# Two-layer hybrid decoder, hand-over from mixer to experts: first head's queries projected from the unscaled state

## What is computed

```python
ada = (c_act @ ada_w[l] + ada_b[l])[:, None, :]
sh1, sc1, g1, sh2, sc2, g2 = jnp.split(ada, 6, axis=-1)
h = rms_norm(x, norm_mix_g[l]) * (1.0 + sc1) + sh1
x = x + g1 * hybrid_mixer(h, ...)
h = rms_norm(x, norm_ffn_g[l]) * (1.0 + sc2) + sh2
x = x + g2 * peer_ffn(h, peer_w_query[l], peer_sub_keys[l], peer_u[l], peer_v[l])

def peer_ffn(h, w_query, sub_keys, u_tab, v_tab):
    q = (xt @ w_query).reshape(T, PEER_HEADS, 2, PEER_DHALF)
    s = jnp.einsum('thpd,pkd->thpk', q, sub_keys).astype(jnp.float32)
    s_a, i_a = lax.top_k(s[:, :, 0], PEER_TOPK)
    s_b, i_b = lax.top_k(s[:, :, 1], PEER_TOPK)
    cand_s = (s_a[..., :, None] + s_b[..., None, :]).reshape(T, PEER_HEADS, n_cand)
    top_s, pos = lax.top_k(cand_s, PEER_TOPK)
    idx = jnp.take_along_axis(cand_i, pos, axis=-1)
    gate = jax.nn.softmax(top_s, axis=-1).astype(h.dtype)
    ...
        u = u_tab[ib]
        act = jax.nn.gelu(jnp.einsum('thkd,td->thk', u, xb), approximate=False)
        return jnp.einsum('thk,thkd->td', gb * act, v_tab[ib])
```

## Time and profile before

| | us |
|---|---|
| median of 3 runs | 2156.43 |
| lowest, highest | 2154.32, 2159.74 |
| profiled execution: time | 2158.78 |
| profiled execution: span of the profile | 2157.0 |
| mean granted TensorE clock | 0.972 |
| bytes moved by DMA | 713.12 MB |
| of these gathered rows | 536.90 MB |

### The profile page before, as it was taken

The page is one execution under the profiler, slowest core; times in us unless marked ns, Lnnn a source line. Parts: engine busy times, 40 slices in busy tenths (PEclk is TensorE's granted clock), DMA queues, the critical chain, the costliest instruction groups (busy, mean ns, idle before and its releaser), DMA issues.

```text
span 2157.0 us, 21974 instructions
## 1 busy us (share of the span) xinstructions
PE 1880.6 (87%) x6340; PEld 1094.4 (51%) x6340; DVE 1481.6 (69%) x4053; ACT 685.5 (32%) x1905; POOL 629.6 (29%) x608
## 2 busy tenths in 40 slices
PE   4999999988888888877799999998978879788776
PEld 3677777654434334433277777775534334334332
DVE  6676686776766767766636676776766766766774
ACT  1222332233333333333322332241333333333332
POOL 5000000144444444444300000002444445444442
PEclk9999999999999999999999999999999999999999
DMA  9855553299999999999986544336999999999997
GB/s 370 326 186 204 215 220 125 114 399 422 419 421 421 421 415 422 409 420 418 411 302 228 205 178 168 127 127 263 400 421 421 418 420 407 422 419 414 406 421 299
DMA packets 118818, 713.12 MB, mean 331 GB/s; under 512 B 13104, under 2 KB 17456, under 8 KB 51120
## 3 DMA queue, kind: packets, MB, share of 16 engines
q0 software_dynamic: 73728, 536.90, 60.2%
q1 hardware_dynamic: 44976, 174.97, 21.6%
HBM read 710.78 MB, written 1.05 MB: 330 GB/s over the span
## 4 chain that ended last, share of the span: by engine, by line
PE 46%; DMA 27%; DVE 15%; issue 4%; ACT 3%; POOL 2%; SPq 2%; DVEq 0%; POOLq 0%; ACTq 0%
DMA wall<-in_peer_uv,idx 23%; PE PS L1192 15%; PE PS L945 11%; PE PS L950 8%; DVE wall L1257 6%; PE PS L955 5%; DMA braw<-in_ada_rows 2%; POOL wall L623 2%; PE PS L1166 2%; ACT M L823 1%; PE PS L992 1%; DVE pos L1742 1%; ACT wgt L816 1%; DVE ts L1739 1%; PE PS L965 1%
## 5 line engine op out<-in xcount | busy, mean ns | idle before, releaser
L1192 PE MATMUL PS<-wall,M 128*128 128x512 f32 x2032 | 954.2, 619 | 214.4 <-ACT M L823 214.0
L1257 DVE CUSTOM_DVE_ANT_0 wall<-wall,tok 128x1024 f32<-128x1024 f32 x512 | 604.7, 1223 | 361.2 <-DMA wall<-in_peer_uv,idx 361.2
L623 POOL DMA_INDIRECT wall<-in_peer_uv,idx x512 | 569.1, 1111 | 714.6 <-PE PS L1192 509.8
L1192 PEld LDWEIGHTS PS<-wall,M 128*128 128x128 f32 x2032 | 384.8, 197 | 744.9 <-issue 412.0
L809 ACT ACTIVATE dg<-dg 128x2 f32<-128x2 f32 x254 | 51.6, 203 | 760.7 <-DVE dg L1257 760.7
L945 PE MATMUL PS<-hT,wall 128*128 128x256 f32 x1120 | 247.9, 380 | 1.3 <-DMA wall<-in_w_in 1.3
L945 PEld LDWEIGHTS PS<-hT,wall 128*128 128x128 f32 x1120 | 211.6, 190 | 31.5 <-ACT M L706 1.7
L565 POOL TENSOR_SCALAR rsb<-ms 128x4 f32<-128x4 f32 (+2 forms) x22 | 6.5, 296 | 756.7 <-DVE ms L1257 755.5
L950 PE MATMUL PS<-wall,hT 128*128 128x512 f32 x512 | 224.7, 592 | 0.2 <-ACT M L692 0.2
L823 ACT ACTIVATE M<-turn,wgt 128x128 f32<-128x128 f32 x508 | 176.2, 394 | 24.1 <-ACT wgt L816 0.7
L950 PEld LDWEIGHTS PS<-wall,hT 128*128 128x128 f32 x512 | 96.1, 190 | 109.3 <-issue 108.5
(11 more groups left out here) (277 smaller groups left out, 1870.8 us busy)
## 6 DMA issues: line engine op xcount, KB each, us to landing
wall<-in_w_in SPq DMA_DIRECT2D x112, 704.0 KB, 9.8
braw<-in_ada_rows SPq DMA_DIRECT2D x72, 512.0 KB, 4.2
wall<-in_w_out SPq DMA_DIRECT2D x2, 4096.0 KB, 14.8
wall<-in_peer_uv,idx POOLq DMA_INDIRECT x512
wall<-in_ada_rows SPq DMA_DIRECT2D x6, 1024.0 KB, 12.4
wall<-in_w_in SPq DMA_DIRECT2D x16, 384.0 KB, 11.0
mix<-in_peer_w_query SPq DMA_DIRECT2D x6, 1024.0 KB
wall<-in_w_in SPq DMA_DIRECT2D x16, 320.0 KB, 9.4
```

The lines of the kernel that those rows point to most:

```text
L623: nc.gpsimd.indirect_dma_start(out=pair_rows[b][s], out_offset=None, in_=uv_rows, in_offset=bass.IndirectOffsetOnAxis(ap=idx[i % 2][:, k:k ...
L1192: ins = mm(bank(B_ACC + 2 * t + hf), diag[:, b, s, :], pair_rows[b][s][:, D + hf * 512:D + (hf + 1) * 512], start=(i == FIRST_TILE[t] and ...
L1257: return v.tensor_tensor_reduce(out=o, in0=a, in1=b, scale=1.0, scalar=0.0, op0=ALU.mult, op1=ALU.add, accum_out=acc)
```

## The change

1. **Columns of a and b.** A new tile `acol` collects, during the mixer, the scale, the shift and the scale of the second norm as columns, two small DVE copies in each `block_out`. (`ccol` is where they were made for the rows `ada`.)
2. **The shift's share.** In `last_step` PE multiplies the shift column with the first head's query matrix (`q0c`, two columns, 16 matmuls of one moving column each); ACT copies them out; later two matmuls spread q0c @ keys over all tokens, in the free half of the bank of the turned keys (`s_shift`).
3. **First head's queries.** PE transposes `xs` as added (L1180), without the reciprocal root; ACT scales each 128x128 block by the scale column as it copies (`raw_evac`). DVE's `best_first` multiplies the scores by the token's root and adds the shift's share. The normed rows are made as before, and `turn_state(0)` with `state_evac(0)` now comes after the whole output projection, for the second head.
4. **The last head.** ACT makes the exponentials before the last sigmoid; DVE's `gates` are split, with the part that needs the sigmoid (`recur_gains`) after `squares`; on PE `levels` stand ahead of `transpose_tok(2)`, six chunks of `out_proj(0, 1)` follow the recurrence, and two chunks (not five) of `out_proj(1, 0)` stand ahead of the hand-over.
5. **Scratch by last use.** The tiles in `mix` are laid out so that a 1 MB third is free after the scores, after the gates, and at the end; four of the five late query matrices are loaded earlier.
6. **First sums.** `expert_sum(0)` comes ahead of the second head's key scores and `gate_rows`, and `expert_sum(1)` ahead of tile 1's transposes; the queries of tile 1 come one group later, and their copies on ACT too.

The diff, cut to its core:

```diff
+        acol = sb("acol", [P, 3 * KC])
+        q0c = sb("q0c", [P, 2])
...
+                sp.wait_ge(s_A, HEADS * (l + 1))
+                load_wq(l, 2, s_ahead)
+                sp.wait_ge(s_gated, l + 1)
+                load_wq(l, 3, s_ahead)
+                load_wq(l, NAHEAD + 2, s_ahead)
                 if l + 1 == DEPTH:
                     load_gain(final_g)
+                sp.wait_ge(s_y_rest, l + 1)
+                load_wq(l, HEADS - 1, s_ahead)
                 sp.wait_ge(s_mix, mixed(l) + HEADS)
-                for h in (*range(2, HEADS - 2), HEADS - 1):
-                    load_wq(l, h, s_ahead)
+                load_wq(l, NAHEAD + 1, s_ahead)
...
+                    if n is None:
+                        act.wait_ge(s_q0c, l + 1)
+                        nc.scalar.activation(q0c[:], bank(B_O)[:, 0:2], ACT.Copy).then_inc(s_q0cev, 1)
+                        nc.scalar.activation(e4[jm][:, :, 3, :], last_unit()[:, :, 1, :], ACT.Sigmoid).then_inc(s_zev, 1)
...
+                def raw_evac():
+
+                    for half in range(2):
+                        act.wait_ge(s_tp, NTP * l + 10 + half)
+                        for k in range(4 * half, 4 * half + 4):
+                            i = nc.scalar.activation(hT[:, k, 0:P], bank(B_H[0][half])[:, k % 4 * P:(k % 4 + 1) * P], ACT.Copy,
+                                                     scale=acol[:, 2 * KC + k:2 * KC + k + 1])
+                        i.then_inc(s_hTa, 1)
+
+                raw_evac()
                 query_evac(0, 0, s_q0, l + 1, s_q0ev)
                 turn_evac(KC - 2, 1, 12)
                 turn_evac(KC - 1, 1, 13)
+                state_evac(0)
...
                 route_exp(0)
+                weigh(0)
                 query_evac(1, 0, s_q1, l + 1, s_q1ev)
...
+                    pe.wait_ge(s_r[1], 16 * l + 16)
+                    for a in range(2):
+                        for k in range(KC):
+                            i = mm(bank(B_O)[:, a:a + 1], wqv[0][:, k, a * P:(a + 1) * P], acol[:, KC + k:KC + k + 1],
+                                   start=(k == 0), stop=(k == KC - 1))
+                    i.then_inc(s_q0c, 1)
                     pe.wait_ge(s_hTa, NHTA * l + 4)
                     pe.wait_ge(s_wo, 16 * (l + 1))
                     out_proj(0, 0, range(4))
+                    pe.wait_ge(s_q0cev, l + 1)
+                    levels(m, jm)
+                    turn_weights(m)
                     pe.wait_ge(s_zev, UNITS * (H0 + HEADS))
                     pe.wait_ge(s_mix, mixed(l) + 6)
                     transpose_tok(2)
-                    levels(m, jm)
-                    turn_weights(m)
                     pe.wait_ge(s_hTa, NHTA * l + 5)
                     out_proj(0, 0, (4, 5))
                     attend(m, jm)
-                    out_proj(0, 1, range(3))
                     pe.wait_ge(s_AH, m + (H0 + 1))
                     recur(m, jm)
                     pool_out(PAIRS - 1, (0,))
-                    out_proj(0, 1, range(3, 6))
+                    out_proj(0, 1, range(6))
...
-                out_proj(1, 0, range(5))
+                out_proj(1, 0, range(2))
...
-                turn_state(0)
-                pe.wait_ge(s_r[1], 16 * l + 16)
+                for half, done in enumerate((s_left, s_raw)):
+                    pe.wait_ge(done, l + 1)
+                    for k in range(4 * half, 4 * half + 4):
+                        i = nc.tensor.transpose(bank(B_H[0][half])[:, k % 4 * P:(k % 4 + 1) * P],
+                                                xs[:, 0, k * P:(k + 1) * P], ident[:])
+                    i.then_inc(s_tp, 1)
+                pe.wait_ge(s_kte, l + 1)
+                for a in range(2):
+                    i = mm(bank(B_KEYS)[:, (2 + a) * P:(3 + a) * P], q0c[:, a:a + 1].to_broadcast([P, P]), keysT[:, a, :],
+                           start=True, stop=True)
+                i.then_inc(s_shift, 1)
...
-                out_proj(1, 0, (5,))
+                out_proj(1, 0, range(2, 6))
                 out_proj(1, 1, range(6))
                 pe.wait_ge(s_hTa, NHTA * l + 10)
                 out_proj(1, 0, (6,))
                 pe.wait_ge(s_hTa, NHTA * l + 11)
                 out_proj(1, 0, (7,)).then_inc(s_wod, 1)
                 out_proj(1, 1, range(6, KC)).then_inc(s_wod, 1)
+                turn_state(0)
...
                     if g == 0:
                         state_evac(1)
-                    if g < 2:
-                        query_evac(g, 1, s_chunk, HEADS * l + g + 1, s_qev)
+                    if g in (1, 2):
+                        query_evac(g - 1, 1, s_chunk, HEADS * l + g, s_qev)
...
-                key_scores(1)
...
                     if g == 0:
+                        key_scores(1)
+                        gate_rows()
+                    elif g == 1:
                         turn_state(1)
-                    if g < 2:
-                        half_queries(g, 1).then_inc(s_chunk, 1)
+                    if g in (1, 2):
+                        half_queries(g - 1, 1).then_inc(s_chunk, 1)
...
+                    ch(copy(acol[:, bass.ds(h * 4 + p * 2, 2)], ccol[:, jm, p, :]))
...
-                    gates(h + 1, 1, g)
+                    gates_ready(h + 1, 5)
+                    pool_gate(1)
+                    attend_gate(1)
                     turned(h + 1)
                     assemble(h + 1)
                     attended(h + 1)
+                    ch(recur_gate(1))
                     recurred(h + 1)
                     squares()
+                    gates_ready(h + 1, 6)
+                    recur_gains(1).then_inc(s_gated, 1)
+                    dve.wait_ge(s_gated, l + 1)
...
-                        if hf == 0:
-                            i.then_inc(s_left, 1)
-                    ch(i)
-                    ch.sync()
+                        i.then_inc((s_left, s_raw)[hf], 1)
+                    dve.wait_ge(s_raw, l + 1)
...
+                    dve.wait_ge(s_shift, l + 1)
+                    ch(copy(cand, bank(B_KEYS)[:, 2 * P:4 * P]))
+                    ch.sync()
                     dve.wait_ge(s_psc0, l + 1)
-                    halves = [bank(B_SC)[:, a * P:(a + 1) * P] for a in range(2)]
+                    ch(stt(cand2, bank(B_SC)[:, 0:2 * P], rs[:, 0:1], cand, ALU.mult, ALU.add))
+                    ch.sync()
+                    halves = [cand2[:, a * P:(a + 1) * P] for a in range(2)]
```

85 lines of the change are left out of this document (51 added, 34 removed).

## The result

| | us |
|---|---|
| before, median of 6 runs | 2156.70 (2153.67 to 2159.74) |
| after, median of 6 runs | 2143.05 (2139.56 to 2148.37) |
| ratio, 95% interval | 0.9943, [0.9933, 0.9952] |
| profiled execution after: time, span | 2141.92, 2140.2 |

The changed kernel is 13.7 us faster. The forecast was 2155.0 with a range from 2148.0 to 2163.5, so the time lies outside the range, on the fast side. The profiled execution of before is one of its slower ones (2158.78), so the two profiles differ by 16.8 us and the medians by 13.7.

A forecast was written before the change was run, and what follows sets the result against it. PE was taken to set the pace up to about 425 us, the DMA from about 480. A gain of 0.7 us per layer, 1.4 in all, took the median 2156.43 to 2155.0, range 2148 to 2163.5.

The forecast's parts named there:

- a group of two rows takes 4.97 us of DMA: In the steady gather stream, a two-row group costs 4.97 us of DMA, a spacing everything behind it keeps.
- DMA takes it all: Rival: routing of both heads stays ahead of DMA, the 12.5 us backlog becomes an earlier stream; 2145 to 2148; chance 0.12.
- (a): In the mixer's last step: q0c's 16 one-column matmuls take 3.5 us on PE; the row behind starts 2.8 later.
- the cheap case: Rival: q0c's matmuls cost only their columns; the gain is 2 to 2.5 us per layer, 2152; chance 0.18.
- cold clock: Rival: PE idles about 2 us before sum(0), which then costs 7.0 us instead of 3.5; 2162; chance 0.16.
- (b): Mixer's last step: exponentials first, three output projection chunks behind recur; the first token tile's projection ends 2.4 us later.
- (c): From that projection's end to the first gather: path 2.2 us shorter, yet the gather comes no earlier, at 430.5.
- (d): Query matrices: four of five issued before the first addition cost nothing; group 0 lands at 439, a 3 us gain.
- the 12 us of backlog removed buy 0.9: At dot(0): despite the DMA backlog removed, it still waits for the first head's gate, 441.1 against 442.00.
- (e): Before dot(0): the first head's gate ends last, behind the whole output projection and a table load, at 441.1.
- (f): dot(0) to dot(9): groups 5 to 7 issued earlier, but group 9 needs sum(4); 0.7 us gained per layer.
- late release: Rival: the unexplained 4.6 us before ACT's copy of half_queries(1, 0) hits turn_state(0); +4.4 per layer, 2165; chance 0.12.

The follow-up runs named there:

- e10: Kernel before with 128 bytes ahead of `wall`, scratch by last use and early loads, plus the second group's sum ahead of tile 1's transposes and projections: 2135.90 us.
- e8: Kernel before with 128 bytes ahead of `wall`, scratch by last use and four of five late query matrices loaded earlier: 2133.78 us.
- e1: Kernel before with an unused tile of 128 bytes per partition ahead of `wall`, no instruction changed: 2138.33 us.
- e3: Kernel before with an unused tile of 384 bytes per partition ahead of `wall`: 2139.58 us.
- e5: Kernel before with an unused tile of 256 bytes per partition ahead of `wall`: 2155.30 us.
- e6: Kernel before with the unused 128 bytes between `wall` and `ring0`, so only the tiles behind `wall` move: 2156.75 us.
- e2: Changed kernel with `acol` and `q0c` allocated behind all other tiles, so `wall` stands where it stood before: 2159.78 us.
- e4: Changed kernel with the five late query matrices issued together behind the mixer, as before the change: 2153.75 us.
- e7: Changed kernel with only 2 of the 16 one-column matmuls, so the first head's scores are wrong: 2137.90 us.
- e9: Changed kernel with the 16 one-column matmuls in four runs of four, one ahead of each of four output projection chunks: 2140.55 us.
- e11: Changed kernel with ACT's exponentials of the first head ahead of its copies of the second head's turned rows: 2138.68 us.

## Why the prediction was right or wrong

**What failed: "a group of two rows takes 4.97 us of DMA", and from it "so a layer gains only what makes the steady stream start earlier".** The time of a group was taken as a constant of the kernel, and the place of its buffers stood at nothing, without a reason. "The scratch tiles laid out by last use change no instruction" is true and was the wrong question: the new tiles `acol` and `q0c` are declared ahead of `wall` and move it by 128 bytes. A group then takes 4.94 us and not 5.00 (577.4 and 585.3 for 117 groups), over 128 groups in each of two layers. The move alone is worth 18 us (2138.33 against 2156.45), more than the whole difference, and with it taken back the changed kernel is at 2159.78. It was in neither the sum nor a rival, and the range could not hold it. The rival "DMA takes it all" gives nearly the right number, 2145 to 2148, but its mechanism, an earlier stream, did not happen: the stream starts later, so its nearness is luck.

**(a) q0c, duration: right.** Forecast 3.5, measured 3.63 to 3.94 in the changed kernel, with its 32 weight loads taking 3.65 to 3.96; the cheap case is out. **(a) q0c, sum: mis-sized.** I priced the matmuls and not what they do to the clock. The rival of the cold clock was placed 50 us later, behind an idle PE; here PE was busy all the time with passes that move one column, and the next chunks ran at half the clock: +3.05 in layer 0 of the changed kernel (6.75 against 3.70). Taking 14 of 16 out gives 5.2 us in all, where my cheap case (2 to 2.5 a layer, not 0.7) gives 2.6 to 3.6. The loads alone, 2 us a layer at the first gather, are near what I had; the rest is the clock.

**(b) and (c): right, where the clock held.** From S to the first gather the changed kernel takes 42.3 us in layer 1, and 42.4 in layer 0 with `wall` moved back, against 41.4 and 41.6 before: +0.8 to +0.9 for a forecast +0.6. In layer 0 of the changed kernel it is 45.8, with the 3.05 in it.

**(d): only half right.** The loads cost no visible time where they went, but taking them away from behind the mixer is worth more than I gave it: 4.6 us in the old order, 10.7 in the new. The term that was mis-sized is "the 12 us of backlog removed buy 0.9": from first gather to dot(0) it is 3 us a layer between the kernels with late and early loads (13.5 and 13.0 against 10.2 and 10.3). Part of the rest in the new order is the clock: with late loads PE waits 5.9 and 5.3 us ahead of sum(0), whose 8 passes then take 6.73 and 5.28 us, against 5.32 and 3.70 in the changed kernel. For the old order no such reading was made.

**(e): right in what ends last, close in number.** From first gather to dot(0) the forecast was 441.1 - 430.5 = 10.6, measured 444.02 - 433.78 = 10.2, and the gate is what ends last. What was off is how far it stands behind the landing of group 0. I had the landing 8.5 us behind the first gather, 2 us ahead of the gate; with the gate out of the way dot(0) starts 9.6 behind it, released by DMA. So the repair is worth 0.6 us a layer at dot(0).

**(f): mechanism right, size missed in the changed kernel.** Layer 0 with `wall` moved back, where neither q0c nor the first sum met a half clock, is the nearest to a clean case: S to dot(4) is 81.0 against 81.2 before (forecast +0.3 to +1.3), and to dot(10) 105.2 against 105.9, 0.7 less, the forecast. That it is met to the tenth is luck. The two layers of before differ by 0.8 themselves (105.9 and 105.1), and the gather of group 9 is 1.4 later than before (forecast +0.2 to +1.1), since sums 4 and 5 met a half clock here as well. But its layer 1, with the half clock, has 107.5 against 105.1, and the changed kernel 110.0 and 105.8. Two things were missing: the half clock in sum(0) (5.32 for 8 passes at 448.04), which I had as a rival, and a second one in sums 4 and 5 (8.83 for 16 passes), which the new order of the sums brings about by leaving PE idle for 3.03 us before them: the order alone, put into the kernel with early loads (e10), takes them from 7.13 to 8.83 in both layers. I did not ask what this wait does to the clock.

**The price of the late release was off by itself.** Where the cold clock's sum takes the 0.7 a layer off, this one takes 0.2; with 0.7 it is +3.9 a layer and 2164, not +4.4 and 2165.

**Late release: not what I feared.** The delay between PE's second projection and its copy by ACT is 4.6 to 6.0 us in the profiles of before, and of the kernels with `wall` 128 and 384 bytes on. It is absent in the profiles with `wall` 256 bytes on and with only the tiles behind it moved, which have the same instructions and the time of before. ACT's copy with `wall` 256 bytes on follows PE's end (438.35) at once:

```profile
438.39 0.38 ACT L790 ACTIVATE M<-PS 128x256 f32<-128x256 f32 x1 [2.94 <-PE PS L1135]
```

It is absent with the early loads too, in the old order (e8 and e10). So it is not fixed by a place in the program. As recorded, e1 and e3, which have it, ran on one chip, and e5, e6, e8 and e10 on another, so it may belong to the chip or to the execution; no run tells. It hides: group 10's gather comes 93.0 and 92.9 us after S in e6, which is without it, and 93.1 before. What it is stays open.

## What to carry to other kernels

When a diff declares a tile, look where the tiles behind it land, above all the destination of the transfers that bound the kernel, and try that place alone before crediting the rest: here 128 unused bytes did more than the change. Read the rate of a DMA-bound stage as a quantity that can change, not as a constant. And price PE work by what it leaves the clock at: here a run of one-column matmuls, or a wait of 3 us on PE, was in most instances paid again in the passes behind it. So try spreading the small ones between large ones, and don't finish a queue of sums early if nothing follows. Last, before a gain is credited to a move, compare the stretch that the move can reach: two profiles differ in the clock of other stretches as well.

## What the runs showed of the hardware

- Gathers of 8 KB rows, 128 to an issue, move 417 or 418 GB/s over the whole stream with the destination at an odd multiple of 128 bytes in the partition, and 421 to 424 GB/s at a multiple of 256. A group then takes 577.4 / 117 = 4.94 us and not 585.3 / 117 = 5.00, which is 8 us in each layer's stream. The two streams explain 16 of the 18 us in the medians; what remains isn't placed. The start-up is no explanation: from S to group 10 it is 92.2 and 92.1 with `wall` 128 bytes on against 93.1 and 93.1, but with `wall` 256 bytes on, without the gain, it is 92.3 and 92.2 as well. The Trainium skill, "DMA: Bandwidth & Descriptors", section "How a descriptor splits into AXI transactions", says that a descriptor is cut at multiples of 256 bytes, and that the bytes from the boundary below its start cost beats of 32 bytes too. By that, an estimate, 8192 bytes that start 128 off take 8 + 31 x 8 + 4 = 260 beats and not 256, 1.6% more; the streams differ by 1.4% (585.3 against 577.4). The size fits; but the page speaks of reads, while here the destination, which is written, moved, and no run here shows the beats themselves.
- 32 passes with one moving column take 3.63 to 3.94 us, about as much as 32 with 128 columns (3.81); in one layer of the kernel with late loads, where the clock fell among them, 4.73.
- Behind or within such a run the granted clock fell to half level in one layer of the changed kernel and one of the kernel with `wall` moved back, and in both of the kernels with late loads and with the exponentials first, 6 of 8 instances; with the matmuls spread out between chunks it fell in none of 4.
- Seven kernels have a wait of 3.03 us on PE ahead of sums 4 and 5 (the changed kernel, e2, e4, e7, e9, e10 and e11). Of their 14 instances 10 took 8.83 us for the 16 passes behind it, one 10.10, and three 7.13 (both layers with the exponentials first, one with 2 of 16 one-column matmuls). The seven kernels with a wait of 0.99 to 1.62 us there took 7.13 in all 14. So the longer wait goes with the lower clock, and isn't a certain cause of it.
